# Two token mixers of a one-core transformer kernel: half of the fifth modulation row earlier, and another order of loads

## The chip, the cores and the metric

The kernel runs on one core of one Trainium2 chip, in one launch. The metric is the device time in microseconds (us). Times of instructions come from one profiled execution of the program, in us from the start of its span.

## The reference

The input is a sequence of 256 tokens by 1024 features, in fp32. A first block of two layers does, in each layer, a SwiGLU feed-forward (1024 to 2816 and back), a token mixer, and a second feed-forward. The mixer projects to 3072 columns, runs retention, dilated attention and stick-breaking attention on them, and projects back. Around each of the three stands a modulation by vectors made from a condition:

```python
mod = cond @ w_ada[l] + b_ada[l]
sh1, sc1, g1, sh2, sc2, g2, sh3, sc3, g3 = jnp.split(mod[:, None, :], N_MOD, axis=-1)
y = _token_mixer(_modulate(x, sh2, sc2), w_in[l], w_out[l])
x = _post_norm(x, y, g2, 1.0, ln_gain[l, 1], ln_bias[l, 1])
y = _swiglu(_modulate(x, sh3, sc3), ffn2_w_gate[l], ffn2_w_up[l], ffn2_w_down[l])
```

A second block follows (attention and pooling, a short convolution, and twice sixteen experts), with modulation vectors of its own. Each vector ("row") is a product of the condition with a 1024 x 1024 matrix, 4 MB. There are 32 of them.

## The kernel before

Each engine has its own instruction stream, written out by hand; semaphores tie them together. All weights come from HBM through the queue of SyncE (SP), whose order is the order of the code, so that a transfer whose wait is not yet met holds back all behind it.

**The rows.** The modulation rows are not made in a place of their own but beside other work: 2 at the start, 5 in each feed-forward, 5 in each mixer (rows 0 to 4 of the mixer here). The 4 MB of a row come in four transfers of 1 MB ("chunks"), which go in turn to the two halves of the buffer `W_mod`; a chunk holds two "blocks" of 128 x 1024. The five rows of a mixer are 20 chunks, numbered 0 to 19, of which chunk 4n + c is the c-th of row n. On VectorE (DVE) `mod_blocks` multiplies a block by its part of the condition and adds it to an accumulator: one TENSOR_SCALAR for the first block of a row (L1670), seven SCALAR_TENSOR_TENSOR for the others (L1672). After the second block of a chunk it signals `mod_freed`, and SP issues the next chunk but one (`mod_chunk`, L447), which waits for that signal:

```python
sp.wait_ge(mod_freed[c % 2], 2 * job + c // 2)
```

When a row's eight blocks are done, TensorE (PE) sums the accumulator over the partitions (`mod_sum`, L762, called as `row_sum(n)` in the mixer), and DVE adds the bias (`mod_row`, L1686).

**The mixer on PE.** `mixer` on PE is an ordered list: the projection to 3072 columns in six groups of 512 (`project(g, t, bank)`, L873, each of the two token tiles in 16 recorded matmuls), between them the attention of six pairs of heads (`scores`, `second`, `values`), then the projection back (`times_rows`, L854). `keep_running` (L736) issues matmuls whose result is not used. The last four steps before the mixer's end are:

```python
times_rows(y_now, at, 0, (0, 1, 2, 3), order).then_inc(acc_t0, 1)
row_sum(4)
times_rows(y_now, at, 1, (0, 1, 2, 3), order, (0,)).then_inc(acc_half, 1)
times_rows(y_now, at, 1, (0, 1, 2, 3), order, (1,)).then_inc(m_pe.sig("out"), 1)
```

**The mixer on DVE.** It is a list too, in which the blocks of rows 0 to 3 stand in pieces between steps of the attention. Row 4 stood in one piece behind the last step, the copy of the retention's result (L2050). Behind it come, before the norm, the low parts of the next feed-forward's first weights (`low_gate_up`, L1822), `plus_bias` (L1742), the bias of row 4 (L1686), and then the norm of token tile 0 and tile 1 (from L1758, ending in L1792), whose results PE turns (`turn_tile`, L783), before the second feed-forward starts (L818).

**The loads.** The projection's weights are 12 transfers of 1 MB (uses 0 to 11, two for each group of 512 columns, L522) into a ring of slots; uses 12 to 15 are the weights of the projection back. `MIX_CHUNKS` says before which use which chunks are issued: `2: (0, 2)` means chunks 0 and 1 stand before use 2. The stream of the second feed-forward follows; it issues its first weights, then chunks 18 and 19, and then waits for the mixer's last matmul.

Of the kernel before, what the change touches and what calls it, by code (L numbers as in the profile page):

```python
# [26 lines left out]
KC = D // P  # L27
# [34 lines left out]
SQUARED = (0, 2, 3, 7, 9)  # L62
SHARED_TURNS = (1, 4, 5, 11)
MIX_BANK = (3, 3, 3, 1, 6)
MIX_CHUNKS = {2: (0, 2), 6: (2, 8), 8: (8, 12), 10: (12, 16), 12: (16, 18)}
SLOTS = 12
SPARE = 7
FEW = 2 * CAP
# [79 lines left out]
def build(nc, A, out):  # L148
    with ExitStack() as ctx:
# [69 lines left out]
        def part(of, at, *shape):  # L219

            n = int(np.prod(shape))
            v = of[:, at:at + n]
            names = "abcd"[:len(shape)]
            if len(shape) > 1:
                v = v.rearrange(f"p ({' '.join(names)}) -> p {' '.join(names)}", **dict(zip(names[:-1], shape)))
            return v
# [195 lines left out]
        def _(sp):  # L422
# [74 lines left out]
            for l in range(LAYERS):  # L497
                ffn_stream(l, 0)

                def mix_chunks(first, end):  # L500
                    for n in range(first, end):
                        mod_chunk(l * JOBS_LAYER + (FIRST_JOBS + PAIRS + n // 4), n % 4, n // 4)
                for u in range(MIX_USES):
                    s = MIX_S[u]
                    if u in MIX_CHUNKS:
                        mix_chunks(*MIX_CHUNKS[u])
                    if u < 2:
# [1147 lines left out]
        def _(dve):  # L1655
            mul, add, sub = ALU.mult, ALU.add, ALU.subtract

            def mod_blocks(job, done, b0, b1, acc=mod_acc):

                for b in range(b0, b1):  # L1660
                    c, kk = b // 2, b % 2
                    if b:
                        dve.drain()
                    if kk == 0 or b == b0:
                        dve.wait_ge(mod_landed[c % 2], job * 32 + 16 * (c // 2 + 1 - 2 * FIRST_JOBS))
                    w = part(W_mod[:, c % 2, :], 0, 2, D)[:, kk, :]
                    col = cond[:, ds(job, 1), b:b + 1].rearrange("p a k -> p (a k)")
                    if b == 0:
                        dve.wait_ge(pe_mod, done + 1)
                        ins = dve.tensor_scalar(acc[:, :], w, col, None, mul)  # L1670
                    else:
                        ins = dve.scalar_tensor_tensor(acc[:, :], w, col, acc[:, :], mul, add)  # L1672
                    if kk:
                        ins.then_inc(mod_freed[c % 2], 1)
# [219 lines left out]
            def mixer(l):  # L1894
                if l == 0:
                    dve.wait_ge(s_mixer_const, 16 * len(MIXER_ONLY))
                def mixer_blocks(n, first=0, end=KC):
                    job = l * JOBS_LAYER + (FIRST_JOBS + PAIRS + n)
                    mod_blocks(job, job - FIRST_JOBS - (1 if n in (1, 2) else 0), first, end, mix_acc[n])
# [79 lines left out]
                def stick_out(b):  # L1979
                    dve.wait_ge(m_pe.s, m_pe.at(f"C{b}", l))  # L1980
                    c = P * (b // 2)
                    dve.tensor_copy(y_tok[:, :, 768 + c:768 + c + P], part(psum[:, 3, :], 0, TT, S)[:, :, c:c + P]
                                    ).then_inc(m_dve.sig(f"y{b}"), 1)

                def decayed(b):
                    dve.wait_ge(m_pe.s, m_pe.at(f"A{b}", l))
                    h = 2 * ATT[b][1]
                    dve.tensor_tensor(att[b % 2][:, :, 0:S], pair(b)[:, :, 0:S], K["decay"][:, h:h + 2, :], mul)
                    dve.tensor_tensor(att[b % 2][:, :, S:3 * P], pair(b)[:, :, S:3 * P], K["decay"][:, h:h + 2, 0:P], mul
                                      ).then_inc(m_dve.sig(f"r{b}"), 1)  # L1990
# [33 lines left out]
                stick_mask(3)  # L2024
                decayed(5)
                stick_out(3)

                dve.wait_ge(m_pe.s, m_pe.at("C5", l))
                for t in range(TT):
# [19 lines left out]
                    dve.wait_ge(tr_pe, (l * 4 + 2) * 4 + b + 3)  # L2049
                    ins = dve.tensor_copy(uT[:, 2 * b:2 * b + 2, :], part(psum[:, 6 + b, :], 0, 2, S))  # L2050
                ins.then_inc(tr_dve, 1)
                mixer_blocks(4)


            for sem_ in (hi_gu, hi_d, lo_gu, lo_d, pe_gu, pe_down, act_silu, dve_h, tr_act, tr_dve, pe_mod):
# [14 lines left out]
            for l in range(LAYERS):  # L2070
                s = 3 * l
                turn_tiles(4 * l, split=True, between=(lambda: None) if l else (lambda: low_gate_up(0, 0, 0)))
                if l == 0:
                    low_gate_up(0, 0, 1)
                    dve.wait_ge(mod_stored, 16 * FIRST_JOBS)
                ffn(l, 0)
                columns(s + 1, (tr_act, 4 * l + 2))
                norm(s, ((acc_t0, s + 1), (pe_down, l * (2 * TILES) + (1 + TILES))), ALPHA, 0.5, LN_EPS)
                turn_tiles(4 * l + 1)
                times_gain(s + 1)  # L2080
                mixer(l)
                for t in range(2):
                    low_gate_up(l, 1, t)
                plus_bias(s + 1)
                mixer_row(l, 4)
                columns(s + 2, (tr_act, 4 * l + 3))
                norm(s + 1, ((acc_t0, s + 2), (acc_half, l + 1), (m_pe.s, m_pe.at("out", l))), ALPHA, 1.0, LN_EPS)
                turn_tiles(4 * l + 3, split=True)
                ffn(l, 1, (1, 0) if l == 0 else None)
                if l == LAYERS - 1:  # L2090
                    dve.engine_nop().then_inc(tr_dve, 1)
                columns(s + 3, (tr_act, 4 * l + 5))
                norm(s + 2, ((acc_t0, s + 3), (pe_down, l * (2 * TILES) + (1 + 2 * TILES))), ALPHA, 0.5, LN_EPS)
# [243 lines left out]
```

## Time and profile before

| | |
|---|---|
| median of 3 runs | 2393.42 us (2393.04 to 2395.78) |
| the profiled execution's own time | 2392.94 us |
| its span in the profile | 2390.7 us |
| mixer of layer 0 on PE, first projection to last matmul | 243.45 to 394.04 us |
| mixer of layer 1 on PE | 812.92 to 962.11 us |
| PE busy over the span | 2162.4 us (90%) |
| DVE busy | 1142.6 us (48%) |
| DMA | 758.16 MB, mean 317 GB/s |

The rows below are lines of the timeline, where "x4" is the number of merged instructions, the second column is the time from the first one's start to the last one's end, and the bracket at the end is the time that the engine sat idle before it, and what ended that. The granted clock is a share of TensorE's full speed.

### The profile page before, as it was taken

Reading aid. Unit: us, or ns where it says so; the run is one execution under the profiler, and the core shown is the slowest. Engines: PE = TensorE matmul, PEld = TensorE weight load, DVE = VectorE, ACT = ScalarE, POOL = GpSimd, SP = SyncE. Lnnn points to the kernel's source line nnn. Section 1 sums busy time; section 2 is a strip of 40 time slices with the busy share of each in tenths; the row PEclk is TensorE's granted clock in tenths of the full one; section 3 lists DMA queues with packets and bytes.
Section 4 is the critical chain, followed back from the end, with each engine's and each line's share of the span. In section 5 each row is a group of like instructions: output and inputs, shape, how many; then the busy total and the mean of one; then the engine's idle time right before and its main releaser. Section 6 shows DMA issues by size and latency. Waiting matters only on the chain.

```text
span 2390.7 us, 35665 instructions
## 1 busy us (share of the span) xinstructions
PE 2162.4 (90%) x13564; PEld 1428.5 (60%) x13564; DVE 1142.6 (48%) x1765; ACT 557.5 (23%) x883; POOL 65.6 (3%) x96
## 2 busy tenths in 40 slices
PE   7999998999999999999999987777779998888886
PEld 5999465999899655799876432222239643333332
DVE  3887767878887875877644210000027421000002
ACT  3343132333433222333332100000023110000001
POOL 0000000000000000000200000000000000000000
PEclk9999998999999999999999999999999999888888
DMA  9986875789688685888834999999997699999996
GB/s 337 341 296 247 303 273 181 271 296 322 232 288 293 249 287 194 277 290 308 283 154 160 356 409 410 410 410 410 410 387 245 266 354 410 409 410 409 410 410 279
DMA packets 290915, 758.16 MB, mean 317 GB/s; under 512 B 17616, under 2 KB 127472, under 8 KB 290720
## 3 DMA queue, kind: packets, MB, share of 16 engines
q1 hardware_dynamic: 283904, 737.34, 82.1%
q0 software_dynamic: 6688, 19.78, 2.7%
q8 instruction: 43, 0.70, 0.1%
q14 instruction: 24, 0.20, 0.0%
q10 hardware_dynamic: 256, 0.13, 0.0%
HBM read 756.01 MB, written 1.18 MB: 317 GB/s over the span
## 4 chain that ended last, share of the span: by engine, by line
PE 56%; DMA 25%; SPq 8%; DVE 6%; ACT 2%; issue 2%; DVEq 1%; ACTq 0%
PE psum L818 21%; DMA W<-in_w_exp_up 12%; PE psum L830 10%; DMA W<-in_w_exp_down 9%; SPq L551 7%; PE psum L1202 3%; DMA W_mod<-in_mod_w 3%; PE psum L1296 3%; PE psum L873 3%; PE psum L854 3%; PE psum L736 2%; PE psum L1251 2%; PE psum L1235 2%; PE psum L1080 1%; DVE mod_acc L1672 1%
## 5 line engine op out<-in xcount | busy, mean ns | idle before, releaser
L818 PEld LDWEIGHTS psum<-parts 128*128 128x128 f32 x4224 | 517.8, 192 | 10.1 <-issue 3.0
L818 PE MATMUL psum<-parts 128*128 128x256 f32 x4224 | 520.9, 283 | 1.8 <-ACT parts L1330 1.5
L1202 PE MATMUL psum<-W,scr 128*32 128x512 f32 x1936 | 248.1, 609 | 70.5 <-DMA W<-in_w_exp_up 67.5
L736 PE MATMUL psum<-k_ones,k_ident 128*128 128x256 f32 x1000 | 281.2, 413 | 0.0
L1672 DVE SCALAR_TENSOR_TENSOR mod_acc<-W_mod,cond,mod_acc 128x1024 f32<-128x1024 f32 x196 | 251.8, 1285 | 47.3 <-issue 27.8
L2215 DVE TENSOR_TENSOR scr<-scr,psum 128x256 f32<-128x256 f32 x32 | 13.5, 421 | 533.9 <-ACT scr L1592 533.9
L736 PEld LDWEIGHTS psum<-k_ones,k_ident 128*128 128x128 f32 x1000 | 182.0, 198 | 143.5 <-issue 125.6
L830 PE MATMUL psum<-parts 128*128 128x512 f32 x1056 | 257.8, 393 | 0.0
L1822 DVE TENSOR_TENSOR parts<-W,parts 128x1024 fp32r<-128x1024 f32 x176 | 207.1, 1219 | 56.5 <-ACT parts L1381 56.4
L1235 PE MATMUL psum<-W,scr 128*32 128x256 f32 x2048 | 160.3, 445 | 77.8 <-DMA W<-in_w_exp_down 61.6
L830 PEld LDWEIGHTS psum<-parts 128*128 128x128 f32 x1056 | 192.6, 188 | 45.3 <-DVE parts L1835 8.2
L1381 ACT ACTIVATE parts<-W 128x1024 fp32r<-128x1024 f32 x176 | 175.8, 1051 | 69.0 <-issue 46.4
L1202 PEld LDWEIGHTS psum<-W,scr 128*32 128x32 f32 x1936 | 46.3, 109 | 208.5 <-DMA W<-in_w_exp_up 138.1
L873 PE MATMUL psum<-W,uT 128*128 128x512 f32 x384 | 168.3, 594 | 0.8 <-issue 0.4
L1235 PEld LDWEIGHTS psum<-W,scr 128*32 128x32 f32 x2048 | 62.1, 123 | 163.0 <-DMA W<-in_w_exp_down 111.5
L2229 DVE COPY scr<-psum 32x256 f32<-32x256 f32 x64 | 27.3, 426 | 267.6 <-PE psum L1235 267.1
L1592 ACT ACTIVATE scr<-psum 128x256 f32<-128x256 f32 x32 | 12.3, 384 | 553.8 <-PE psum L1202 553.8
L873 PEld LDWEIGHTS psum<-W,uT 128*128 128x128 f32 x384 | 71.5, 190 | 86.4 <-issue 86.4
L1400 ACT ACTIVATE gate_att<-psum 128x256 f32<-128x256 f32 x88 | 33.8, 384 | 369.0 <-PE psum L818 369.0
L1251 PE MATMUL psum<-scr 128*128 128x512 f32 x256 | 117.5, 602 | 0.8
L1835 DVE TENSOR_TENSOR parts<-W,parts 128x1024 fp32r<-128x1024 f32 x88 | 107.2, 1219 | 10.3 <-ACT parts L1393 10.3
L1393 ACT ACTIVATE parts<-W 128x1024 fp32r<-128x1024 f32 x88 | 92.9, 1056 | 43.6 <-PE psum L830 43.6
(312 smaller groups left out, 1784.8 us busy)
## 6 DMA issues: line engine op xcount, KB each, us to landing
W<-in_w_exp_down SPq DMA_DIRECT2D x128, 1024.0 KB
W_mod<-in_mod_w SPq DMA_DIRECT2D x123, 1024.0 KB, 5.8
W<-in_w_exp_gate SPq DMA_DIRECT2D x242, 512.0 KB, 14.5
W<-in_w_exp_up SPq DMA_DIRECT2D x242, 512.0 KB, 15.7
W<-in_ffn_w_gate SPq DMA_DIRECT2D x44, 1024.0 KB, 8.6
W<-in_ffn_w_up SPq DMA_DIRECT2D x44, 1024.0 KB, 11.0
W<-in_ffn_w_down SPq DMA_DIRECT2D x44, 1024.0 KB, 9.7
W<-in_w_in SPq DMA_DIRECT2D x24, 1024.0 KB, 8.6
```

The source lines that it names most:

```text
L551: sp.dma_start(to[:, D * n:D * n + D], w[layer, ds(e, 1), P * b:P * b + P, :] .rearrange("a p n -> p (a n)")).then_inc(done, 16)
L736: pe.matmul(psum[:, bank, 0:256], ident[:, :], K["ones"][:, :].unsqueeze(1).to_broadcast([P, 2, P]), start=True, stop=True, skip_group_che ...
L818: ins = pe.matmul(psum[:, 4 + t % 2, S * g:S * g + S], w[:, t % 2, g, kc, :], u[:, kc, :], start=(n == 0 and kc == 0), stop=(n == 2 and kc ...
L830: ins = pe.matmul(psum[:, 2 * tt + h, :], h_[:, t % 2, P * tt:P * tt + P], w[:, t % 2, 512 * h:512 * h + 512], start=(t == 0 and n == 0), ...
L873: ins = pe.matmul(psum[:, bank, :], uT[:, kc, P * t:P * t + P], part(W[:, s, :], 0, 4, 512)[:, kc % 4, :], start=(kc == 0), stop=(kc == KC ...
L1202: ins = pe.matmul(psum[32 * q:32 * q + 32, 4, :].rearrange("p (g n) -> p g n", g=2), xe_now[:, b, :], w[:, :, q, :], start=(b == 0), stop= ...
L1235: ins = pe.matmul(psum[32 * q:32 * q + 32, 6, 0:256], e_hT[:, c % 2, 32 * (c // 2):32 * (c // 2) + 32], part(W[:, s, :], 0, 2, D)[:, c % 2 ...
L1251: ins = pe.matmul(psum[:, 2 * tt + h, :], GT[:, P * tt:P * tt + P], R[:, 512 * h:512 * h + 512], start=first, stop=True, skip_group_check= ...
L1381: ins = act.activation(gu_hi[:, t % 2, g, :, :], part(W[:, b + g, :], 0, KC, STEP)[:, :, P * (t % 2):P * (t % 2) + P], copy)
L1672: ins = dve.scalar_tensor_tensor(acc[:, :], w, col, acc[:, :], mul, add)
L1822: ins = dve.tensor_tensor(gu_lo[:, t % 2, g, :, :], part(W[:, b + g, :], 0, KC, STEP)[:, :, P * (t % 2):P * (t % 2) + P], gu_hi[:, t % 2, ...
L1835: dve.tensor_tensor(d_lo[:, t % 2, :], part(W[:, b + 2, :], 0, 2, D)[:, t % 2, :], d_hi[:, t % 2, :].bitcast(F32), sub).then_inc(lo_d, 1)
```

## The change

The order of loads in the mixers changes, and the first four of the eight blocks of row 4 stand before the wait for the last attention step, C5, instead of at the end.

```diff
-MIX_CHUNKS = {2: (0, 2), 6: (2, 8), 8: (8, 12), 10: (12, 16), 12: (16, 18)}
+MIX_CHUNKS = {2: (0, 2), 6: (2, 6), 8: (6, 10), 9: (10, 12), 10: (12, 14), 11: (14, 16), 12: (16, 18)}
...
                 stick_mask(3)
                 decayed(5)
                 stick_out(3)
+                mixer_blocks(4, 0, 4)

                 dve.wait_ge(m_pe.s, m_pe.at("C5", l))
...
                 ins.then_inc(tr_dve, 1)
-                mixer_blocks(4)
+                mixer_blocks(4, 4, KC)
```

Both layers run this code. No instruction and no transfer is added or removed.

## Rows read from the trace of the kernel before

**Rows 1.** The page: the chain that ended last, by engine.

```profile
PE 56%; DMA 25%; SPq 8%; DVE 6%; ACT 2%; issue 2%; DVEq 1%; ACTq 0%
```

**Rows 2.** Timeline of PE, end of the mixer of layer 0 (start us, us, what).

```profile
368.57 1.04 PE L1005 MATMUL psum<-k_ident,tmp 128*128 128x128 f32 x8
...
372.88 7.03 PE L854 MATMUL psum<-W,uT 128*128 128x512 f32 x16
383.42 1.08 PE L762 MATMUL psum<-mod_acc,k_ones 128*32 128x256 f32 x8 [3.52 <-DVE mod_acc L1672]
384.44 9.60 PE L854 MATMUL psum<-W,uT 128*128 128x512 f32 x16
397.55 1.97 PE L783 MATMUL psum<-k_ident,x_tok 128*128 128x128 f32 x8 [3.51 <-DVE x_tok L1792]
...
404.64 1.04 PE L783 MATMUL psum<-k_ident,x_tok 128*128 128x128 f32 x8
```

**Rows 3.** Timeline of DVE, the same stretch.

```profile
358.46 1.68 DVE L2031 BATCH_NORM_STATS2 stats<-psum 128x6 f32<-128x128 f32 x8 [9.07 <-PE psum L938]
...
370.41 0.75 DVE L1670 TENSOR_SCALAR mod_acc<-W_mod,cond 128x1024 f32<-128x1024 f32 x1
...
377.76 2.64 DVE L1672 SCALAR_TENSOR_TENSOR mod_acc<-W_mod,cond,mod_acc 128x1024 f32<-128x1024 f32 x2 [2.51 <-DMA W_mod<-in_mod_w]
380.73 2.64 DVE L1672 SCALAR_TENSOR_TENSOR mod_acc<-W_mod,cond,mod_acc 128x1024 f32<-128x1024 f32 x2 [0.32 <-DMA W_mod<-in_mod_w]
383.29 4.62 DVE L1822 TENSOR_TENSOR parts<-W,parts 128x1024 fp32r<-128x1024 f32 x4
...
391.77 1.23 DVE L1758 TENSOR_TENSOR tmp<-psum,gate_att 128x1024 f32<-128x1024 f32 x1
...
403.14 0.81 DVE L1792 TENSOR_SCALAR x_tok<-tmp,mv,inv 128x1024 f32<-128x1024 f32 x1
```

**Rows 4.** Timeline of the SP queue, layer 0.

```profile
258.66 0.37 SPq L447 DMA_DIRECT2D W_mod<-in_mod_w  x1
...
269.05 1.01 SPq L522 DMA_DIRECT2D W<-in_w_in  x2
272.77 0.37 SPq L447 DMA_DIRECT2D W_mod<-in_mod_w  x1
...
334.62 0.37 SPq L447 DMA_DIRECT2D W_mod<-in_mod_w  x1
...
348.07 3.34 SPq L478 DMA_DIRECT2D W<-in_ffn_w_down  x1
```

**Rows 5.** All 120 chunks of the mixers and feed-forwards (line L447): issue to landing.

```profile
DMA to landing us min/median/max: 4.7/5.8/13.6
```

**Rows 6.** Timeline of DVE, layer 0: last blocks of row 1, first of row 2.

```profile
273.91 2.65 DVE L1672 SCALAR_TENSOR_TENSOR gate_att<-W_mod,cond,gate_att 128x1024 f32<-128x1024 f32 x2 [1.17 <-DMA W_mod<-in_mod_w]
...
283.34 0.75 DVE L1670 TENSOR_SCALAR mod_acc<-W_mod,cond 128x1024 f32<-128x1024 f32 x1 [6.45 <-DMA W_mod<-in_mod_w]
```

**Rows 7.** Timeline of PE, layer 0: the sum of row 1.

```profile
278.71 0.64 PE L762 MATMUL psum<-gate_att,k_ones 128*32 128x256 f32 x8
```

**Rows 8.** Timeline of DVE, end of the mixer of layer 1.

```profile
939.96 0.74 DVE L1670 TENSOR_SCALAR mod_acc<-W_mod,cond 128x1024 f32<-128x1024 f32 x1
...
952.82 4.62 DVE L1822 TENSOR_TENSOR parts<-W,parts 128x1024 fp32r<-128x1024 f32 x4
...
972.31 0.81 DVE L1792 TENSOR_SCALAR x_tok<-tmp,mv,inv 128x1024 f32<-128x1024 f32 x1
```

**Rows 9.** Timeline of PE, layer 1: the sum of row 2, the turn of tile 1.

```profile
866.33 0.64 PE L762 MATMUL psum<-mod_acc,k_ones 128*32 128x256 f32 x8 [0.56 <-DVE mod_acc L1672]
...
974.41 1.04 PE L783 MATMUL psum<-k_ident,x_tok 128*128 128x128 f32 x8
```

**Rows 10.** Windows around a turn in the second block (stretch, PE, PEld, DVE, ACT, POOL, PEclk, DMA).

```profile
1784.60:1787.10 2.50, 0.11 (x1) 0.00 (x0) 0.95 (x2) 2.49 (x4) 0.00 (x0) 1.00 1.10 352
...
1789.00:1790.00 1.00, 1.00 (x7) 1.00 (x6) 0.81 (x3) 0.97 (x4) 1.00 (x2) 0.50 1.10 348
```

## The prediction

> **What bounds the kernel now.** I read the page first. Its chain that ended last is mostly PE and DMA [rows 1]: PE through the first block and DMA through the experts. DVE is only 6% of it, and the change touches only the DVE's list and the order of SP's loads, so the question is whether those 6% contain the work that moves. I then took the timelines of PE, DVE and SP over the mixer of layer 0. PE is dense there for 136 us, until the fifth row's sum. There PE sits idle for 3.52 us, released by the DVE's accumulation [rows 2]. The wait is for row 4: DVE starts its first block at 370.41 us, and leaves the row at 383.29 us, after 12.88 us, of which 2.51 and 0.32 us are waits for the last two chunks [rows 3]. Nor is PE the bound after this. PE waits again for 3.51 us for the first normalised tile [rows 2], and the DVE runs from 383.29 to 403.95 us with no gap above half a microsecond, through the low parts, the bias and the norm. So from 370.4 us to the turn of tile 1 at 404.64 us, the DVE's list sets the end, and row 4 stands at its head. Layer 1 shows the same: 939.96 to 952.82 us, or 12.86 us [rows 8].
>
> **The moved blocks.** Blocks 0 to 3 of row 4 cost one 0.75 us instruction and three of 1.32 us (2.64 us for two), 4.8 us with the gaps [rows 3]. Their new place is where DVE sat idle for 9.07 us, from 349.39 to 358.46 us, waiting for PE's last attention step [rows 3]. They end at 354.2 us, 4.2 us before the cover ends. They need chunks 16 and 17. The later, chunk 17, is issued at 334.62 us [rows 4]; even with the longest landing of all chunks, 13.6 us [rows 5], it is there at 348.2 us. The sum of row 3, which reads the same accumulator, stands before in PE's list, and the bias of row 3 before in DVE's. So the four blocks cost nothing where they go. If the cover were gone they would cost their 4.8 us, as they do today.
>
> **The moved transfers.** Chunks 18 and 19 wait for the buffers that blocks 1 and 3 free. That is now about 352 and 354 us, not 372.5 and 375 us. SP reaches them after the feed-forward's down weights, whose issue takes until 351.4 us [rows 4], so it is not late. Seven transfers of 1 MB stand in the queue ahead of them. Allowing the longest landing of 13.6 us [rows 5], chunk 19 is there by 368.5 us, before DVE wants it at 370.5 us (more likely at 360). So the 2.51 and 0.32 us of waiting go too. Behind the two chunks SP waits for the mixer's last matmul, so nothing is held back.
>
> **The sum at the end of a mixer.** After the change DVE has four blocks left, 4 x 1.32 us and 0.1 us of gaps, 5.4 us. It leaves row 4 at 375.8 us instead of 383.29 us: 7.5 us earlier, and 7.5 us in layer 1. What is late next? PE finishes the matmuls before the sum at 379.9 us, so its 3.52 us stall is gone. The sum takes 0.6 us and the last 16 matmuls 7.0 us at the rate of the 16 before it [rows 2] (they now take 9.60 us, because the clock has dropped during the stall), so PE ends at 387.4 us. DVE wants the sum of row 4 at 382.6 us (2.1 us of slack), tile 0 at 384.3 us (there since 379.9) and the last half tile at about 392 us (4.5 us of slack). The DVE's list stays the bound, with no new wait in it, and all of its 7.5 us arrive at the turn of tile 0. From there PE carries the feed-forward, which starts earlier by the same amount. The first weights of its loop wait for PE's end, 6.7 us earlier, and are wanted 7.5 us earlier, so their lead over their use shrinks by 0.8 us; with two of them landing about 6 us after issue like a chunk [rows 5], and some 95 matmuls of the feed-forward before their use, I count nothing for it.
>
> **The turn of tile 1.** The tile is written at 403.95 us but PE turns it at 404.64 us, held by its own filler at half the clock. In layer 1 it is 973.12 against 974.41 us [rows 2, 3, 8, 9]. If the clock stays full after the shorter idle time (387.4 to 390 us, 2.6 us, instead of 3.51 us), 0.6 and 1.2 us come on top; if it falls, nothing. Before, both idle times of 3.5 us are followed by half clock. One of 2.5 us in the second block kept the full clock at first and was at 0.50 about 2 us later [rows 10]. So this is a toss-up, worth 0 to 1.8 us, and I take half.
>
> **The new order of loads.** Uses 6 and 7 now go out behind chunk 5, at about 259 us instead of 269.05 us. Use 8 goes before chunk 10, use 9 before chunk 12, use 10 before chunk 14. No projection weight is issued later than before. The chunks are what can be late. Before, chunk 8 stood behind two weight loads and landed 10.6 us after its issue (272.77 to 283.34 us), and DVE sat 6.45 us for it [rows 4, 6]. That wait cost PE only 0.5 us, at the sum of row 2 (0.56 us in layer 1 [rows 9]). With the loads out earlier, row 2 starts about 4 us sooner, and this stall goes: 0.5 us per layer. In exchange chunks 6 and 7 now stand behind the loads. From the loads' issue to the landing of the chunk behind them took 14.3 us before (269.05 to 283.34). Counted from 259.1 us this gives chunk 6 at 273.4 us; its blocks end at 276.0 us, those of chunk 7 at 278.7 us, and PE wants the sum of row 1 at 278.71 us [rows 7]. So even this bound costs nothing. If chunk 7 itself landed 10.6 instead of the median 5.8 us after issue, 4.8 us late against its 273.91 us [rows 6], DVE would finish at 281.3 us and PE would stall 2.6 us per layer. I take zero, the bound that follows the loads' own issue.
>
> The Trainium skill, "DMA: Bandwidth & Descriptors", section "Queues, rings and completion order", speaks against this part: descriptors are consumed in ring order and a semaphore's increment waits for every earlier write on that engine, so that a chunk can't pass the weight loads. The 10.6 us above, nearly twice the median, agree. By its table in "Bandwidth" (1 MB at 341 GB/s) the five transfers from chunk 5 to chunk 7 would take 15.4 us from 258.66, an estimate that puts chunk 7 at 274.1 us, 0.2 us later than now, and would leave the sum unchanged.
>
> **The total.** 2 x 7.5 + 2 x 0.5 + 0.9 = 16.9 us. The profiled execution took 2392.9 us, so 2376.0 us. It stands 0.5 us below the median of the three runs, so I forecast 2376.5 us, 0.7% below before. The later phases are tied to PE's events through semaphores, so I expect them to move as a whole.
>
> **The rivals.**
> The forecast, 78%: 2374.5 to 2378.5 us, the clock deciding within it.
> Chunks 6 and 7 stall row 1's sum, 8%: up to 2.6 us a layer are lost, 2377 to 2382 us. For it speaks that chunk 8 was 10.6 us under way; against it that the loads have 6 us more of a start on chunk 6 than the bound needs.
> The second half still waits for its chunks, 5%: the 2.8 us of waits stay in each layer, about 2382 us. This takes landings of more than 16 us, and none of 120 was over 13.6 us [rows 5].
> The gain is given back later, 4%: the feed-forward's loop or the experts' loads don't start earlier and the time stays at 2389 to 2397 us. For it speaks the experts' share of DMA in the chain; against it that its loads are released by PE.
> Slower, 2%: chunk 17 lands so late that the early blocks hold the DVE past PE's last attention step. They hold it from a landing at 355.8 us on (2.65 us for two blocks before 358.46). The gain of 8 us a layer is used up at 364 us, 29 us after the issue, and at 367 us it costs 3 us a layer: 2399 us.
> Still faster than 2374.5 us, by more stalls that go than I counted, 3%.
>
> **The range.** 2372 to 2381.5 us holds the forecast, most of the stall at row 1 and the faster side. By 0.2% (4.8 us), about what a measurement of this kernel can tell from no change, faster is 0.94, same 0.04, slower 0.02.
>
> **What the profile would show.** Right: the DVE's idle time before the retention's statistics falls from 9.07 to about 4.2 us in both layers; SP issues chunks 18 and 19 some 20 us earlier; no idle time of PE before the sum of row 4, and full clock in the 16 matmuls behind it; the mixer's last matmul 7 us after the sum; the turn of tile 0 about 8 us earlier, with 2.6 us of idle time before it. The DVE's wait at the first block of row 2 is about 2 us, not 6.45. Wrong: a wait of PE at the sum of row 1 (the loads were in the way), a wait of the DVE for W_mod at block 4 or 6 of row 4, or a first feed-forward matmul that is earlier while the experts' first load isn't.

## The result, and the profile after

| | before | changed |
|---|---|---|
| median of 4 runs each | 2393.57 us (2393.04 to 2395.78) | 2373.77 us (2373.07 to 2374.78) |
| profiled execution: time, span | 2392.94, 2390.7 us | 2373.07, 2370.9 us |

The ratio of the times is 0.9916, with a 95% interval of 0.9899 to 0.9933: 16.0 to 24.2 us faster. The forecast was 2376.5 us, in a range of 2372 to 2381.5 us. The medians differ by 19.8 us; the sum had 16.9 us.

The first question is whether the stall at the end of a mixer went, and what took its place. The timeline of PE in layer 0 of the changed kernel answers to [rows 2]:

```profile
367.83 1.04 PE L1005 MATMUL psum<-k_ident,tmp 128*128 128x128 f32 x8
...
372.14 7.03 PE L854 MATMUL psum<-W,uT 128*128 128x512 f32 x16
379.10 0.64 PE L762 MATMUL psum<-mod_acc,k_ones 128*32 128x256 f32 x8
379.67 7.13 PE L854 MATMUL psum<-W,uT 128*128 128x512 f32 x16
389.40 1.50 PE L783 MATMUL psum<-k_ident,x_tok 128*128 128x128 f32 x8 [2.60 <-DVE x_tok L1792]
390.70 4.93 PE L736 MATMUL psum<-k_ones,k_ident 128*128 128x256 f32 x16
395.87 1.09 PE L783 MATMUL psum<-k_ident,x_tok 128*128 128x128 f32 x8 [0.24 <-DVE x_tok L1792]
396.80 2.33 PE L736 MATMUL psum<-k_ones,k_ident 128*128 128x256 f32 x10
399.39 12.11 PE L818 MATMUL psum<-parts 128*128 128x256 f32 x96 [0.27 <-ACT parts L1330]
```

The sum of row 4 follows the matmuls before it without idle time, and the 16 matmuls behind it take 7.13 us instead of 9.60 us. The turn of tile 0 starts at 389.40 us after 2.60 us of idle time; before it was 397.55 us after 3.51 us. The turn of tile 1 moved from 404.64 to 395.87 us. In layer 1 the turn of tile 0 has the same idle time before it and takes less:

```profile
950.32 1.09 PE L783 MATMUL psum<-k_ident,x_tok 128*128 128x128 f32 x8 [2.60 <-DVE x_tok L1792]
```

DVE in the same stretch, answering to [rows 3]:

```profile
348.58 0.74 DVE L1670 TENSOR_SCALAR mod_acc<-W_mod,cond 128x1024 f32<-128x1024 f32 x1
349.39 4.01 DVE L1672 SCALAR_TENSOR_TENSOR mod_acc<-W_mod,cond,mod_acc 128x1024 f32<-128x1024 f32 x3
357.73 1.68 DVE L2032 BATCH_NORM_STATS2 stats<-psum 128x6 f32<-128x128 f32 x8 [4.32 <-PE psum L938]
...
368.47 1.29 DVE L2051 COPY uT<-psum 128x512 f32<-128x512 f32 x2 [3.60 <-PE psum L1005]
369.85 5.38 DVE L1672 SCALAR_TENSOR_TENSOR mod_acc<-W_mod,cond,mod_acc 128x1024 f32<-128x1024 f32 x4
375.15 4.62 DVE L1822 TENSOR_TENSOR parts<-W,parts 128x1024 fp32r<-128x1024 f32 x4
...
383.62 1.22 DVE L1758 TENSOR_TENSOR tmp<-psum,gate_att 128x1024 f32<-128x1024 f32 x1
...
395.00 0.81 DVE L1792 TENSOR_SCALAR x_tok<-tmp,mv,inv 128x1024 f32<-128x1024 f32 x1
```

The four early blocks fill half of the idle time before the statistics: 9.07 us became 4.32 us, and PE still releases them (L938). Row 4 is left at 375.15 us, 8.1 us earlier than before, and neither half waits for `W_mod`. Of these 8.1 us, 0.7 us were won before this stretch (357.73 against 358.46 us), 0.2 us of them already before the mixer began.

SP's queue in layer 0, answering to [rows 4]:

```profile
258.99 1.02 SPq L522 DMA_DIRECT2D W<-in_w_in  x2
265.16 0.37 SPq L447 DMA_DIRECT2D W_mod<-in_mod_w  x1
...
347.37 3.34 SPq L478 DMA_DIRECT2D W<-in_ffn_w_down  x1
350.75 0.71 SPq L447 DMA_DIRECT2D W_mod<-in_mod_w  x1
...
354.01 0.44 SPq L447 DMA_DIRECT2D W_mod<-in_mod_w  x1
```

Chunks 18 and 19 go out at 350.75 and 354.01 us, some 22 us earlier. Chunk 6, the one that now stands behind two weight loads, goes out at 265.16 us. On DVE, answering to [rows 6]:

```profile
271.68 5.38 DVE L1672 SCALAR_TENSOR_TENSOR gate_att<-W_mod,cond,gate_att 128x1024 f32<-128x1024 f32 x4 [3.81 <-DMA W_mod<-in_mod_w]
...
279.28 0.75 DVE L1670 TENSOR_SCALAR mod_acc<-W_mod,cond 128x1024 f32<-128x1024 f32 x1 [1.89 <-DMA W_mod<-in_mod_w]
```

The wait moved, as forecast, from the first block of row 2 (6.45 to 1.89 us) to chunk 6 (3.81 us), and it does not reach PE: row 1 is done at 276.97 us, and PE sums it, without idle time, at 278.53 us (it was 278.71 us [rows 7]).

**Where the 20 us came from.** Marks on PE in the two profiled executions, us:

| | before | changed | changed minus before |
|---|---|---|---|
| first projection of layer 0 | 243.45 | 243.26 | -0.2 |
| second feed-forward of layer 0 starts (L818) | 408.11 | 399.39 | -8.7 |
| second feed-forward of layer 1 starts | 977.88 | 959.93 | -17.95 |
| last matmul group L818 of the first block starts | 1163.6 | 1145.6 | -18.0 |
| first experts' matmul (L1202) | 1317.64 | 1298.84 | -18.8 |
| first L1235 | 1328.3 | 1307.8 | -20.5 |
| last L1235 | 2372.7 | 2352.9 | -19.8 |

All that the change does is won by 960 us: 17.95 us, of which 0.2 us lie before the first mixer, so 17.8 us for the two layers (8.5 and 9.2 us). The other 1.8 us appear in code that is the same in both kernels: 0.8 us won ahead of the first expert and 1.7 us in it, 0.7 us lost behind it. Windows of the first expert's gate and up (stretch, PE, PEld, DVE, ACT, POOL, granted clock, DMA share, GB/s), before:

```profile
1317.00:1328.20 11.20, 9.58 (x68) 3.24 (x68) 2.77 (x9) 1.15 (x3) 0.00 (x0) 0.85 0.68 249
```

and changed:

```profile
1298.50:1307.70 9.20, 7.88 (x68) 2.79 (x68) 2.46 (x8) 0.84 (x3) 0.00 (x0) 1.00 0.63 216
```

The same 68 matmuls took 9.58 us at a granted clock of 0.85 and 7.88 us at 1.00. Whether that belongs to the change is tested last.

### The profile page after: what moved, and what is told of

The parts are those of the page before. It is cut to its first block, busy times and chain, and to the rows that moved or that the text cites. A ratio compares the mean times of both kernels' runs of the same rounds, so it can differ in the third digit from the quotient of the medians.

```text
span 2370.9 us, 35665 instructions
## 1 busy us (share of the span) xinstructions
PE 2165.7 (91%) x13564; PEld 1427.8 (60%) x13564; DVE 1142.9 (48%) x1765; ACT 556.9 (23%) x883; POOL 65.3 (3%) x96
## 4 chain that ended last, share of the span: by engine, by line
PE 58%; DMA 19%; SPq 14%; DVE 4%; issue 2%; ACT 2%; DVEq 1%; ACTq 0%
PE psum L818 21%; DMA W<-in_w_exp_up 16%; SPq L551 11%; PE psum L830 10%; PE psum L873 7%; PE psum L1202 3%; PE psum L1296 3%; PE psum L854 3%; DMA W<-in_w_exp_down 2%; PE psum L1080 1%; PE psum L736 1%; SPq L555 1%; PE psum L1235 1%; PE psum L1251 1%; PE psum L762 1%
## 5 line engine op out<-in xcount | busy, mean ns | idle before, releaser
L818 PEld LDWEIGHTS psum<-parts 128*128 128x128 f32 x4224 | 517.8, 192 | 10.1 <-issue 3.0
L818 PE MATMUL psum<-parts 128*128 128x256 f32 x4224 | 520.9, 283 | 1.8 <-ACT parts L1330 1.5
L1202 PE MATMUL psum<-W,scr 128*32 128x512 f32 x1936 | 244.2, 605 | 68.2 <-DMA W<-in_w_exp_up 65.1
L2216 DVE TENSOR_TENSOR scr<-scr,psum 128x256 f32<-128x256 f32 x32 | 13.5, 421 | 527.6 <-ACT scr L1592 527.6
L1235 PE MATMUL psum<-W,scr 128*32 128x256 f32 x2048 | 171.1, 469 | 68.4 <-DMA W<-in_w_exp_down 52.2
L1202 PEld LDWEIGHTS psum<-W,scr 128*32 128x32 f32 x1936 | 47.2, 109 | 201.2 <-DMA W<-in_w_exp_up 133.1
L1235 PEld LDWEIGHTS psum<-W,scr 128*32 128x32 f32 x2048 | 64.2, 127 | 161.2 <-DMA W<-in_w_exp_down 105.8
## 6 DMA issues: line engine op xcount, KB each, us to landing
W<-in_ffn_w_up SPq DMA_DIRECT2D x44, 1024.0 KB, 10.9
```

The costliest lines, as they stand in the source:

```text
L818: ins = pe.matmul(psum[:, 4 + t % 2, S * g:S * g + S], w[:, t % 2, g, kc, :], u[:, kc, :], start=(n == 0 and kc == 0), stop=(n == 2 and kc ...
L1202: ins = pe.matmul(psum[32 * q:32 * q + 32, 4, :].rearrange("p (g n) -> p g n", g=2), xe_now[:, b, :], w[:, :, q, :], start=(b == 0), stop= ...
L1235: ins = pe.matmul(psum[32 * q:32 * q + 32, 6, 0:256], e_hT[:, c % 2, 32 * (c // 2):32 * (c // 2) + 32], part(W[:, s, :], 0, 2, D)[:, c % 2 ...
```

## The experiments

The theory is that of the prediction: row 4 at the end of DVE's list sets the turn of tile 0; the half that moves is worth some 7.5 us a layer because idle time covers it and its chunks come in time; the order of loads is worth some 0.5 us a layer. Each kernel was run beside the kernel before on the same chip, whose median was 2393.11 us in the first set and 2393.43 us in the second. The first four kernels below are one set, the others the second; the changed kernel's 2373.77 us were measured apart from both, beside 2393.57 us for the kernel before. Times of a layer run from its first projection to its second feed-forward (L818).

**The half alone.** The blocks as in the changed kernel, the loads as before.

```diff
-MIX_CHUNKS = {2: (0, 2), 6: (2, 6), 8: (6, 10), 9: (10, 12), 10: (12, 14), 11: (14, 16), 12: (16, 18)}
+MIX_CHUNKS = {2: (0, 2), 6: (2, 8), 8: (8, 12), 10: (12, 16), 12: (16, 18)}
```

> The first four blocks of row 4 early, the loads in the old order. My theory (the blocks left the DVE's list where it set the end) gives 7.5 us a layer and what the clock adds: 0.990 to 0.994 of the time before, 2374 to 2379 us, with PE's 0.56 us wait at the sum of row 2 still there. The rival (the early half only pays because the new order brings the chunks sooner) gives waits of the DVE for W_mod in the early blocks and under half of the gain, above 2384 us.

Measured: 2374.79 us, ratio 0.9922 [0.9908, 0.9936]. Its DVE in layer 0:

```profile
349.71 0.74 DVE L1670 TENSOR_SCALAR mod_acc<-W_mod,cond 128x1024 f32<-128x1024 f32 x1
...
358.86 1.68 DVE L2032 BATCH_NORM_STATS2 stats<-psum 128x6 f32<-128x128 f32 x8 [4.31 <-PE psum L938]
...
370.98 5.38 DVE L1672 SCALAR_TENSOR_TENSOR mod_acc<-W_mod,cond,mod_acc 128x1024 f32<-128x1024 f32 x4
```

No block of row 4 waits for a chunk with the old order either: it is the early blocks that free the buffers. Layer 0 takes 156.89 us, 7.8 us less than before (164.66), while the changed kernel takes 156.13 us. PE still waits at the sum of row 2, 0.69 us in layer 0 and 1.00 us in layer 1, as expected. The half is nearly all of the change: 7.8 and 8.1 us in the two layers, where the changed kernel gains 8.5 and 9.2 us.

**The order alone.** The new `MIX_CHUNKS`, and `mixer_blocks(4)` at the end as before.

```diff
-                mixer_blocks(4, 0, 4)
...
-                mixer_blocks(4, 4, KC)
+                mixer_blocks(4)
```

> The new order of loads alone, row 4 in one piece at the end. My theory: only the wait of PE at the sum of row 2 goes, 0.5 us a layer, so 2392 to 2393 us, not to be told from before by its time; in the trace the sum of row 2 starts without a wait, and the 3.5 us wait at the sum of row 4 stays. The rival (the 2.9 us by which the change beat the forecast come from the order) gives 2389 to 2391 us.

Measured: 2392.45 us, ratio 0.9997 [0.9988, 1.0006]. In time this is no change. In the trace, layer 0 is 0.9 us shorter (163.75 us), and the end of the mixer is as it was, with the stall in front of the sum:

```profile
383.88 1.08 PE L762 MATMUL psum<-mod_acc,k_ones 128*32 128x256 f32 x8 [3.71 <-DVE mod_acc L1672]
```

PE's wait at the sum of row 2 (0.48 and 0.56 us before) is gone in both layers, but not all of the 0.9 us is that. At the turn of tile 0 layer 0 is 0.35 us ahead, since DVE's waits for chunks 18 and 19 grew from 2.83 to 3.03 us. The other 0.6 us come at the turn of tile 1: the filler before it took 4.15 us instead of 5.49 us and no longer held PE. So the term of 0.5 us a layer is about right for the stall, and is too small for a measurement of its own.

**Two more blocks early.** If DVE's list is the bound, blocks 4 and 5 of row 4 should be worth more ahead of the second idle time, the 3.60 us before the copies of `uT`.

```diff
+                mixer_blocks(4, 4, 6)
                 for b in range(2):
                     dve.wait_ge(tr_pe, (l * 4 + 2) * 4 + b + 3)
...
-                mixer_blocks(4, 4, KC)
+                mixer_blocks(4, 6, KC)
```

> Two more blocks of row 4 (4 and 5) moved, into the DVE's 3.6 us wait for the turned retention result. If the DVE's list still sets the end, the norm starts 2.6 us earlier less a wait of about 0.5 us for PE's sum of row 4: 2 to 2.6 us a layer, 0.9975 to 0.9985 of the changed kernel, 2368 to 2370 us. If PE's list has taken over behind the sum, nothing is gained against the changed kernel's 2373.8 us.

Measured: 2370.25 us, ratio 0.9902 [0.9887, 0.9917]. Two lines of DVE and one of PE:

```profile
366.11 2.65 DVE L1672 SCALAR_TENSOR_TENSOR mod_acc<-W_mod,cond,mod_acc 128x1024 f32<-128x1024 f32 x2
369.61 1.29 DVE L2052 COPY uT<-psum 128x512 f32<-128x512 f32 x2 [0.86 <-PE psum L1005]
```

```profile
388.41 1.09 PE L783 MATMUL psum<-k_ident,x_tok 128*128 128x128 f32 x8 [0.46 <-DVE x_tok L1792]
```

The idle time before the copies falls from 3.60 to 0.86 us, and PE's before the turn of tile 0 from 2.60 to 0.46 us. Layer 0 takes 154.03 us, another 2.1 us less. Moving 2.65 us of blocks does not give all 2.65 us: DVE now waits 0.50 us for the sum of row 4, as PE comes close to being the bound.

**All eight blocks before the last attention step.** Where does the cover end? The whole row stands before the wait for C5.

```diff
-                mixer_blocks(4, 0, 4)
+                mixer_blocks(4, 0, KC)
...
-                mixer_blocks(4, 4, KC)
```

> The whole of row 4 ahead of the wait for C5, so that the cover of 4.3 us is exceeded. The later chunks are issued at about 351 and 354 us behind 7 MB, and land at 358 to 361 us; the blocks end at about 363 us, 5 us behind C5, of which 3 us are covered by PE's own matmuls, and PE stalls 2 us a layer; in exchange four more blocks are gone from the end, so the time comes out within 2 us of the changed kernel's 2373.8 us. The rival (a held C5 goes through to the end in full, as the slower case of the forecast has it) gives 8 to 12 us more than the changed kernel.

Measured: 2387.3 us, ratio 0.9979 [0.997, 0.9988], 13.5 us slower than the changed kernel. The theory's expectation of a small difference fell, and even the rival's was too small. DVE, then PE, in layer 0:

```profile
362.78 5.38 DVE L1672 SCALAR_TENSOR_TENSOR mod_acc<-W_mod,cond,mod_acc 128x1024 f32<-128x1024 f32 x4 [8.17 <-DMA W_mod<-in_mod_w]
368.07 1.68 DVE L2032 BATCH_NORM_STATS2 stats<-psum 128x6 f32<-128x128 f32 x8
...
389.71 0.42 DVE L1686 TENSOR_TENSOR mod_out<-psum,mod_bias 128x256 f32<-128x256 f32 x1 [4.94 <-PE psum L762]
```

```profile
358.72 10.47 PE L854 MATMUL psum<-W,scr 128*128 128x512 f32 x24
375.27 1.97 PE L1005 MATMUL psum<-k_ident,tmp 128*128 128x128 f32 x8 [6.08 <-DVE tmp L2048]
377.03 5.18 PE L854 MATMUL psum<-W,scr 128*128 128x512 f32 x8
```

DVE waits 8.17 us for chunk 18, which lands 10.9 us after its issue at 351.90 us, not the median of 5.8 us. This is the chunk behind seven loads, four for the projection back and three for the feed-forward; in the changed kernel it is wanted only at 369.85 us, and its delay costs nothing. Counted from the first projection, the statistics start 9.2 us later than in the changed kernel, and PE's idle time before L1005 is 6.08 us, with half the clock behind it at first: 8 matmuls in 1.97 us instead of 1.04, the next 8 in 5.18 instead of 3.60 us. PE comes 8.8 us late to its matmuls from `uT` (L854). What I had left out is that little makes this up: only the 2.60 us of PE's idle time before the turn of tile 0 can shrink (to 0.46 us), while DVE's list, now short, waits 4.94 us for PE. Layer 0 loses 7.7 us and layer 1 6.0 us.

**The late chunks put back.** The new order and blocks, but SP waits with chunks 18 and 19 until DVE has copied `uT`, at 370.92 and 371.96 us, where they went out at 372.54 and 375.84 us before.

```diff
                 if k == 1:
+                    sp.wait_ge(tr_dve, l * 4 + 4)
                     for c in (2, 3):
```

> The changed kernel, but SP holds chunks 18 and 19 until the retention's result is copied, at about 370 us in layer 0. My theory splits the gain of a layer into 4.8 us of moved blocks and 2.8 us of earlier chunks: with the chunks late, the DVE waits 5 us for chunk 18 and a little for chunk 19, ends row 4 at 380 instead of 375 us, and the time is 8 to 12 us above the changed kernel, 2382 to 2386 us. If only the moved blocks counted, it would stay at 2374 us.

Measured: 2388.46 us, ratio 0.9976 [0.9967, 0.9985], 14.7 us slower than the changed kernel. DVE and PE (lines stand one further down in this kernel):

```profile
375.86 2.64 DVE L1673 SCALAR_TENSOR_TENSOR mod_acc<-W_mod,cond,mod_acc 128x1024 f32<-128x1024 f32 x2 [4.97 <-DMA W_mod<-in_mod_w]
379.88 2.65 DVE L1673 SCALAR_TENSOR_TENSOR mod_acc<-W_mod,cond,mod_acc 128x1024 f32<-128x1024 f32 x2 [1.38 <-DMA W_mod<-in_mod_w]
```

```profile
382.58 0.64 PE L763 MATMUL psum<-mod_acc,k_ones 128*32 128x256 f32 x8 [2.28 <-DVE mod_acc L1673]
...
396.70 1.97 PE L784 MATMUL psum<-k_ident,x_tok 128*128 128x128 f32 x8 [6.42 <-DVE x_tok L1793]
```

The waits add up to 4.97 + 1.38 = 6.35 us, and each layer loses 6.2 us against the changed kernel, 12.4 us of the 14.7 us; what the other 2.3 us are is not shown, and the last experiment finds differences of that size in untouched stretches. The loss is above the 8 to 12 us expected, which counted less of the waits. Against the kernel before, layer 0 is still 2.3 us shorter (162.36 against 164.66 us): 0.5 us is the stall at the sum of row 2, 1.3 us is what the moved half is worth when its chunks don't move, 4.8 us of blocks less 3.5 us of longer waits (6.35 against 2.83 us), and 0.5 us comes at the turn of tile 1, which PE's filler holds for 0.17 instead of 0.69 us. So most of a layer's gain hangs on the early blocks freeing the buffers of chunks 18 and 19.

**The weights first.** Uses 6 to 9 all ahead of chunk 6, to see what a delay of row 1 costs.

```diff
-MIX_CHUNKS = {2: (0, 2), 6: (2, 6), 8: (6, 10), 9: (10, 12), 10: (12, 14), 11: (14, 16), 12: (16, 18)}
+MIX_CHUNKS = {2: (0, 2), 6: (2, 6), 10: (6, 14), 11: (14, 16), 12: (16, 18)}
```

> The changed kernel, with uses 8 and 9 also ahead of chunk 6. They must wait for the fifth projection step's slots (p41, about 271 us), and hold chunks 6 and 7 back in SP's queue from 265 to 272 us; behind 2 MB these land at 279 to 282 us. PE then waits 5 to 7 us at the sum of row 1 (layer 0: from 278.5 us), and some of it comes back where PE waited before: 8 to 14 us above the changed kernel for both layers. The other theory, that the chunks' place in the order is worth nothing as long as the weights are early, gives the changed kernel's 2374 us.

Measured: 2401.06 us, ratio 1.0034 [1.0024, 1.0044], 27 us slower than the changed kernel, about twice the upper end of what was expected. SP in layer 0:

```profile
259.77 1.02 SPq L522 DMA_DIRECT2D W<-in_w_in  x2
...
272.82 0.92 SPq L522 DMA_DIRECT2D W<-in_w_in  x2
273.78 0.50 SPq L447 DMA_DIRECT2D W_mod<-in_mod_w  x1
```

What SP waited for between the two pairs of loads (us in total, times, longest):

```profile
SPq L522 <- PE psum L873: 12.0, 1, 12.0
```

DVE, then PE:

```profile
283.40 5.38 DVE L1672 SCALAR_TENSOR_TENSOR gate_att<-W_mod,cond,gate_att 128x1024 f32<-128x1024 f32 x4 [14.75 <-DMA W_mod<-in_mod_w]
```

```profile
265.65 14.00 PE L873 MATMUL psum<-W,uT 128*128 128x512 f32 x32
289.26 1.08 PE L762 MATMUL psum<-gate_att,k_ones 128*32 128x256 f32 x8 [9.61 <-DVE mod_out L1686]
291.18 8.89 PE L873 MATMUL psum<-W,uT 128*128 128x512 f32 x16
```

SP issues two of the four loads at once and then waits 12.0 us for PE, whose matmuls free the slots of the other two, so chunk 6 goes out 8.6 us later than in the changed kernel. It lands 9.6 us after its issue, and PE stands 9.61 us at the sum of row 1. I had priced the stall alone. Counted from the first projection, the sum of row 1 starts 9.7 us later than in the changed kernel, and what follows the 16 projection matmuls behind it 12.4 us later: the rest is the clock, 8.89 us for 16 matmuls that take 7.03 us at full clock, and 1.08 us for a sum that takes 0.64 us. It stays at that: layer 0 loses 12.4 us (168.57 against 156.13 us) and layer 1 12.6 us, 25 of the 27 us.

This is the stall at the sum of row 1 that a rival forecast, brought about in another way: the rival had chunk 7 land late, here SP holds chunks 6 and 7 back. It shows that the stall costs 1.3 us for each us, where the rival had 1 (2.6 us a layer). The changed kernel misses it by 1.5 us (row 1 done at 276.97 against 278.53 us).

**The bias in the idle time too.** If DVE's list sets the turn until PE becomes the bound, 2.35 us of `plus_bias` (it needs nothing of the mixer's result) can fill the rest of the 4.32 us before C5, and the bias of row 4 can stand between the two tiles. This is on top of the two more blocks early.

```diff
-            def norm(s, summed, alpha, res, eps, last=False):
+            def norm(s, summed, alpha, res, eps, last=False, between=lambda: None):
...
                     scaled(0)
+                    between()
...
                 mixer_blocks(4, 0, 4)
+                plus_bias(3 * l + 1)
...
-                plus_bias(s + 1)
-                mixer_row(l, 4)
                 columns(s + 2, (tr_act, 4 * l + 3))
-                norm(s + 1, ((acc_t0, s + 2), (acc_half, l + 1), (m_pe.s, m_pe.at("out", l))), ALPHA, 1.0, LN_EPS)
+                norm(s + 1, ((acc_t0, s + 2), (acc_half, l + 1), (m_pe.s, m_pe.at("out", l))), ALPHA, 1.0, LN_EPS,
+                     between=lambda: mixer_row(l, 4))
```

> As six_early, with plus_bias (2.35 us) also moved into the DVE's wait for C5, behind the four early blocks, and the bias of row 4 put between the norms of tile 0 and tile 1. If the DVE's list still sets the end, tile 0's norm starts when its sums are there (380.3 instead of 382.6 us): 2 us a layer on top of six_early, about 2366 us. If PE is the bound by now (its last matmuls end at 387.8 us), tile 0 is turned no earlier than that, but tile 1 still 2 us earlier, so the time is the same 2366 us; only if the wait moves to another place is it six_early's 2370 us.

Measured: 2366.43 us, ratio 0.9893 [0.9876, 0.9911]. PE at the turn:

```profile
380.47 7.13 PE L854 MATMUL psum<-W,uT 128*128 128x512 f32 x16
387.44 1.04 PE L783 MATMUL psum<-k_ident,x_tok 128*128 128x128 f32 x8
```

There is no idle time before the turn of tile 0: PE is the bound there, and DVE waits 0.99 us for it (at L1758). Work taken from ahead of that wait would bring tile 0 no earlier. Tile 1 is still set by DVE: PE sits idle for 0.65 us before it in layer 0 and 0.34 us in layer 1. Layer 0 takes 152.05 us, 2.0 us less than with the two more blocks alone. The time does not tell the two theories apart, since both expected 2366 us; the trace does. By the medians this kernel is 27 us faster than the kernel before and 7.3 us faster than the changed one; its range of 2366.19 to 2370.6 us lies below all runs of the changed kernel.

**The changed kernel once more.** Nothing edited, to see whether the 1.7 us of the first expert belong to the change.

> The changed kernel once more, for the stretch that it does not touch, from the last feed-forward to the experts. Theory: the granted clock falls there or not from execution to execution, so the first expert's gate and up matmuls take 9.0 us (as in the changed kernel's profile) or 10.6 to 10.7 us (as before and in four experiments) whatever the change is; then 2 us of the difference of the two profiled spans are not the change's. The rival (the shift by 18 us puts them at full clock) gives 9.0 us again.

Measured: 2378.79 us, span 2376.6 us. The window of its first expert:

```profile
1302.50:1313.50 11.00, 9.58 (x68) 3.24 (x68) 2.57 (x8) 0.92 (x3) 0.00 (x0) 0.84 0.71 243
```

The same program takes 9.58 us for the 68 matmuls, as the kernel before did, at a clock of 0.84. The time from the first L1202 to the first L1235 is 10.6 us here, 10.7 us before, and 10.6 to 10.7 us in the profiles of the other seven experiments; the 9.0 us of the changed kernel's first profile are the only ones of the kind. The gain of 1.7 us in the first expert is a matter of the execution, not of the change.

The part that belongs to the change repeats. From the first projection of layer 0 to the second feed-forward of layer 1 it took 734.43 us before, 716.67 us in the changed kernel and 716.74 us here: 17.8 and 17.7 us less. The 5.7 us by which this span is longer than the first one lie elsewhere: 2.0 us before the first projection (245.25 against 243.26 us), 2.0 us between the last L818 and the first L1202, and 1.6 us in the first expert. In layer 1 the turn of tile 0 has the same 2.60 us before it as in the first profile, and runs at half the clock:

```profile
952.38 1.97 PE L783 MATMUL psum<-k_ident,x_tok 128*128 128x128 f32 x8 [2.60 <-DVE x_tok L1792]
```

## Why the prediction was right, step by step

- **The moved blocks cost nothing.** Right: 4.32 us of idle time remain (forecast 4.2). The half alone is 0.9922 of the time before.
- **The two waits for chunks go.** Right. Chunk 18 took 10.9 us from issue to landing in the trace where DVE stood waiting for it, within the bound of 13.6 us. Putting them back cost 6.2 us a layer for 6.35 us of waits on DVE (layer 0).
- **The sum's stall goes, DVE's list stays the bound, with 7.5 us a layer.** Right. PE has 2.60 us of idle time before tile 0, the number forecast, and two more edits that shorten DVE's list alone go on paying, until that idle time is zero.
- **The stall at row 2's sum, 0.5 us a layer.** Right in the trace: the stall was 0.48 to 1.00 us with the old order and is gone with the new one, with the early half or without. The order alone made layer 0 0.9 us shorter, but 0.6 us of that is the filler before the turn of tile 1. It is below what the time can show.
- **The new order costs nothing at row 1.** Right, by 1.5 us. Chunk 6 landed at 271.68 us where the bound had 273.4, row 1 was done at 276.97 where it had 278.7. Row 2's first block began at 279.28 us. By the table of the Trainium skill, "DMA: Bandwidth & Descriptors", section "Bandwidth", chunk 7 would have come at 274.1 us, an estimate this trace doesn't contradict, for DVE runs the four blocks from 271.68 us without a wait, and the third of them, chunk 7's first, starts about 274.3 us. That a chunk can't pass the loads ahead of it, as the prediction took it from the Trainium skill, "DMA: Bandwidth & Descriptors", section "Queues, rings and completion order", fits the two cases where DVE stood waiting: 10.9 us behind seven loads, and 9.6 us behind two issued 1 us before it.
- **The turn of tile 1, 0 to 1.8 us, taken at 0.9.** This is the term that was mis-sized. The two layers gained 8.5 and 9.2 us, together 17.8 us; 2 x 7.5 + 2 x 0.5 + 1.8 is 17.8, so the whole of the term came, and the prediction had taken half of it. In layer 0 the clock did fall (the turn took 1.50 and the filler 4.93 us, against 1.09 and 3.62 us with two more blocks early, behind 0.46 us of idle time), but part way, and the filler ended before tile 1 was written at 395.81 us; PE turned it 0.06 us later. The condition I had set, full clock or no gain, was too strict: it is enough that the filler ends before the tile is there.
- **The total.** 16.9 us were forecast, 17.7 to 17.8 us is what the change is worth in the traces, and 19.8 us is the difference of the medians and also of the profiled spans; in the spans the other 2 us are in code that the change does not touch, and 1.7 us of them went away when the same kernel was profiled again. Both 16.9 and 17.8 us lie in the measured 16.0 to 24.2 us. The median of 2373.77 us lies in the stated range, but below the 2374.5 to 2378.5 us of the branch with 78%, in the one with 3% ("more stalls that go than I counted"). The runs show no such stall: it is the 0.9 us of the turn of tile 1 and the untouched code. The same kernel then took 2378.79 us, above the branch. A branch 4 us wide was narrower than the spread of executions of the one kernel (2373.07 to 2378.79 us), and that the median still lies in the range is owed to the width given to it for the other rivals.
- **The gain is given back later.** It was not. The experts' first load (L551) went out at 1202.30 us, before at 1219.92 us, 17.6 us earlier: their queue is tied to PE, as argued.
- **The price of an overrun before C5**, 1 us lost for 1 us of delay, was argued only. With all eight blocks there, waiting for chunk 18, the statistics are 9.2 us late, PE is 8.8 us late at its matmuls from `uT`, and the layers lose 7.7 and 6.0 us; the idle time before the turn of tile 0 takes up 2.1 us of it. That is the mechanism, at a price under the one argued. Chunk 17 itself, the rival's case, was late in no run.

## What to carry to other kernels

When a list on one engine sets the end of a stage, look in the same list for idle time that another engine ends, and move there what has its inputs; with double buffers the moved work also starts the transfers behind it earlier, and here the moved half would have won only 1.3 us a layer without that. Before moving it, compare the last landing it needs with the moment the idle time ends: four blocks fitted with 4.3 us to spare, and eight cost 13.5 us. Stop when the engine that waited has no idle time left, and compare marks on the engine that ends last rather than end times, since two executions of the same program differed by 1.6 to 2.0 us in each of three untouched stretches, 5.7 us in all.

## What the runs showed of the hardware

- Long idle time of PE is paid for again behind it. After 6.08 us of idle time 8 matmuls of 128 columns took 1.97 us instead of 1.04, after 9.61 us 16 matmuls of 512 took 8.89 us instead of 7.03. That is the lower of TensorE's two levels, 1.2 instead of 2.4 GHz, for the first of them. A stall of 9.61 us cost a layer 12.4 us. After the stalls of some 3.5 us at the sum of row 4, the 16 matmuls behind it took 9.60 and 8.15 us before and 8.25 us in layer 0 with the order alone, instead of 7.13 us; after 2.28 us (the late chunks) they took 7.13 us.
- After 2.60 us the outcome varied. In the changed kernel the turn took 1.50 us in layer 0 and 1.09 us in layer 1, in the next execution of the same program 1.27 and 1.97 us, each with 2.60 or 2.61 us ahead of it. The layers' times did not follow it (156.13 and 155.75 us, then 156.18 and 155.75 us), since the filler ends before tile 1 is there or just with it.
- The same program's clock is not the same in each execution: 68 matmuls of the first expert took 7.88 us in one profile and 9.58 us in the next, and the two executions differ by 5.7 us in time (2373.07 and 2378.79 us). Runs of the kernel before went from 2387.47 to 2399.82 us.
- How long a 1 MB transfer on SP's queue takes from issue to landing depends on what was issued ahead of it and how long before. It took 6.5 us behind two loads issued 6 us earlier (chunk 6, 265.16 to 271.68 us), 9.6 us behind two issued 1 us earlier (the weights first), 10.6 us behind two issued 3.7 us earlier and a chunk just ahead of them (chunk 8 before), and 10.9 us behind seven. Among those seven, SP stood 10.19 us over the issue of one load (338.23 us), where most take about 0.5 us, and from 340 us until chunk 18 landed the share of busy DMA engines was 1.02 to 1.10.
